# Writing the first stage of a float32 transformer trunk out by hand, pacing a gather, dropping the accumulator clears and halving the tail

## The reference: two macaron layers on 256 tokens

```python
for l in range(2):
    x = x + 0.5 * swiglu(rms_norm(x, ffn1_norm[l]), ffn1_w_gate[l], ffn1_w_up[l], ffn1_w_down[l])
    h = rms_norm(x, mix_norm[l]);  z = h @ w_in[l]          # 1024 -> q | k | v | p, 512 each
    a = neighborhood_attention(q, k, v, rpb[l])             # 8 heads of 64, 2-D windows, learned bias
    m = multiscale_pool(p, w_pool[l], pool_scale[l])
    x = x + concat([a, m]) @ w_out[l]
    x = x + 0.5 * swiglu(rms_norm(x, ffn2_norm[l]), ffn2_w_gate[l], ffn2_w_up[l], ffn2_w_down[l])
return rms_norm(x, final_norm)
# swiglu(h, g, u, d) = (silu(h @ g) * (h @ u)) @ d, with 2816 hidden columns
```

## Time and profile before

| | |
|---|---|
| median of 3 executions | 987.61 us (985.65 to 989.18) |
| profiled execution: span from the first to the last instruction | 983.4 us |
| median less that span (what lies around it) | 4.2 us |
| TensorE busy | 958.7 us, 97% |
| VectorE, ScalarE, GpSimd busy | 552.3, 499.5, 45.1 us |
| DMA | 174.75 MB, mean 178 GB/s |

### The profile page before, as it was taken

One profiled execution on the slowest core, in us unless ns is written; L12 is line 12 of the kernel. 1 busy time (PEld: TensorE's weight loads), 2 busy tenths in 40 slices (PEclk: granted clock), 3 DMA queues, 4 the chain that ended last, 5 costly groups with the idle time before them and its releaser, 6 DMA issues.

```text
span 983.4 us, 13937 instructions
## 1 busy us (share of the span) xinstructions
PE 958.7 (97%) x4390; PEld 780.2 (79%) x4390; DVE 552.3 (56%) x865; ACT 499.5 (51%) x812; POOL 45.1 (5%) x86
## 2 busy tenths in 40 slices
PE   5989999999999999999989999999999999999996
PEld 4878888877788888888878888888868888888885
DVE  4556555467545665554466556564665565465644
ACT  4555455455625654544375545454664365454542
POOL 0550000010001000000010000000100010000000
PEclk9999999999999999999999999999999999999999
DMA  8998646527223746465367555644542266556441
GB/s 285 234 244 284 211 171 212 173 87 250 93 86 129 244 147 210 167 213 171 129 208 254 193 191 171 209 160 143 171 172 86 86 209 199 190 170 213 145 156 43
DMA packets 123269, 174.75 MB, mean 178 GB/s; under 512 B 8240, under 2 KB 99552, under 8 KB 122976
## 3 DMA queue, kind: packets, MB, share of 16 engines
q1 hardware_dynamic: 117328, 165.17, 50.1%
q0 software_dynamic: 2848, 6.38, 3.0%
q10 hardware_dynamic: 3056, 2.75, 0.8%
HBM read 173.14 MB, written 4.19 MB: 180 GB/s over the span
## 4 chain that ended last, share of the span: by engine, by line
issue 92%; POOL 4%; DMA 2%; PE 1%; ACT 0%; ACTq 0%; DVE 0%; POOLq 0%; DVEq 0%; SPq 0%
POOL bias_scratch L364 3%; POOL rstd L337 1%; DMA bias_scratch<-in_rpb_dram 1%; DMA w_raw<-in_ffn_w_up_dram 1%; POOL mean_eps L334 0%; PE ps L868 0%; POOL rstd_scaled L340 0%; PE ps L869 0%; ACT w_hi L416 0%; PE ps L918 0%; ACT L416 0%; POOL bias L371 0%; DVE normed L850 0%; DVEq L95 0%; ACT xt_hi L431 0%
## 5 line engine op out<-in xcount | busy, mean ns | idle before, releaser
L631 DVE SCALAR_TENSOR_TENSOR w_lo<-w_raw,gain,w_hi 128x512 fp32r<-128x512 f32 x416 | 285.4, 746 | 104.3 <-ACT w_hi L416 103.7
L860 PE MATMUL ps<-w_hi,xt_hi 128*128 128x512 f32 x848 | 338.3, 399 | 2.9 <-DVE w_lo L631 2.8
L861 PE MATMUL ps<-w_lo,xt_hi 128*128 128x512 f32 x848 | 330.4, 390 | 0.0
L863 PE MATMUL ps<-w_hi,xt_lo 128*128 128x512 f32 x848 | 326.2, 391 | 0.0
L416 ACT ACTIVATE w_hi<-w_raw,gain 128x512 fp32r<-128x512 f32 x416 | 265.7, 713 | 99.7 <-PE ps L863 78.2
L623 DVE TENSOR_TENSOR w_lo<-w_raw,w_hi 128x1024 fp32r<-128x1024 f32 x104 | 122.7, 1222 | 121.2 <-ACT w_hi L410 121.1
L860 PEld LDWEIGHTS ps<-w_hi,xt_hi 128*128 128x128 f32 x848 | 159.3, 188 | 39.1 <-DVE w_lo L631 4.7
L863 PEld LDWEIGHTS ps<-w_hi,xt_lo 128*128 128x128 f32 x848 | 159.2, 188 | 34.2
L861 PEld LDWEIGHTS ps<-w_lo,xt_hi 128*128 128x128 f32 x848 | 159.6, 188 | 30.4
L410 ACT ACTIVATE w_hi<-w_raw 128x1024 fp32r<-128x1024 f32 x104 | 104.4, 1052 | 105.0 <-PE ps L863 104.3
L860 PE MATMUL ps<-w_hi,gt_hi 128*128 128x512 f32 x352 | 140.0, 398 | 0.0
(11 more groups left out here) (82 smaller groups left out, 468.3 us busy)
## 6 DMA issues: line engine op xcount, KB each, us to landing
w_raw<-in_ffn_w_gate_dram SPq DMA_DIRECT2D x88, 512.0 KB, 4.0
w_raw<-in_ffn_w_up_dram SPq DMA_DIRECT2D x88, 512.0 KB, 5.1
w_raw<-in_ffn_w_down_dram SPq DMA_DIRECT2D x88, 512.0 KB, 4.0
w_raw<-in_w_in_dram SPq DMA_DIRECT2D x32, 512.0 KB, 4.7
w_raw<-in_w_out_dram SPq DMA_DIRECT2D x16, 512.0 KB, 5.2
bias_scratch<-in_rpb_dram POOLq DMA_DIRECT2D x32, 96.0 KB, 6.7
bias<-bias_scratch POOLq DMA_DIRECT2D x2, 1536.0 KB, 8.0
pool_m<-in_pool_matrix_dram ACTq DMA_DIRECT2D x1, 1024.0 KB, 6.5
```

The source lines that it names most:

```text
L631: nc.vector.scalar_tensor_tensor(w_lo[slot][:, part], w_raw[slot][:, part], g, w_hi[slot][:, part].bitcast(F32), ALU.mult, ALU.subtract).t ...
L860: nc.tensor.matmul(o, hi, wh, start=start, stop=False)
L861: nc.tensor.matmul(o, hi, wl, start=False, stop=False)
L863: last = nc.tensor.matmul(o, lo, wh, start=False, stop=stop)
```

## The change

The first gated stage is written out on its own: x is loaded in halves, the weights of chunk 0 in slices (each with its own semaphore), the residual is not added to zeros, both token tiles do the first half of K before the second, and the gains of the first norm are transposed apart from the others. Eight matmuls with zeros stand ahead instead of five. An ACTIVATE with Silu on one column stands ahead of all other work on ACT. The layer loop is a Python loop, so the program is written out for both layers (the chunk loop stays, now from 2). The banks are opened by the first down product of a stage instead of by zeros. The gathers are issued two a chunk, those of layer 0 during its first gated stage, those of layer 1 during its second. Tables and pooling parameters are loaded after the chunk loop of the first gated stage. The second pass enters its first stage with both weight splits on ACT ahead of `xt_hi`. `acc_ready` is raised per bank. In the last stage tile 1 finishes one bank before the other, and the norm behind it is done by halves.

```diff
-            sp.dma_start(resid[:, 0, :], x[0, 0:P, :]).then_inc(x_loaded[0], 16)
-            with sp.Fori(0, DEPTH) as layer:
-                load_ff(layer, FF1, (ffn1_w_gate, ffn1_w_up, ffn1_w_down))
+            def load_first(layer, ff, weights):
+                def quarter(a, k0, k1, q):
+                    slot = ff["g"][a]
+                    dst = w_raw[slot][:, :].rearrange("p (k m c) -> p k m c", k=4, m=2)
+                    for m, w in enumerate(weights[:2]):
+                        src = w[layer, a * 512 + k0 * P:a * 512 + k1 * P, 0:FC]
+                        sp.dma_start(dst[:, k0:k1, m, :], src.rearrange("(k p) c -> p k c", p=P)
+                                     ).then_inc(first_raw[q], 16)
+                sp.dma_start(resid[:, 0, 0:512], x[0, 0:P, 0:512]).then_inc(x_half_loaded, 16)
+                quarter(0, 0, 1, 0)
+                sp.dma_start(resid[:, 0, 512:], x[0, 0:P, 512:]).then_inc(x_loaded[0], 16)
+                for k in range(1, 4):
+                    quarter(0, k, k + 1, k)
+                sp.dma_start(resid[:, 1, :], x[0, P:2 * P, :]).then_inc(x_loaded[1], 16)
+                quarter(1, 0, 2, 4)
+                quarter(1, 2, 4, 5)
+            load_first(0, FF1, (ffn1_w_gate, ffn1_w_up))
+            for layer in range(DEPTH):
+                load_ff(layer, FF1, (ffn1_w_gate, ffn1_w_up, ffn1_w_down), begun=layer == 0)
...
-            for layer in range(DEPTH):
-                for rq in range(P // GRID_W):
-                    for h in range(N_HEADS):
+            def gather_rows(layer, ff, number):
+                for i in range(N_HEADS):
+                    pool.wait_ge(g0_used, chunk_no(layer, ff, i) + 1)
+                    for rq in range(P // GRID_W):
...
+            rstd_of(0)
+            gather_rows(0, FF1, 0)
+            load_bias(0, N_HEADS)
+            rstd_of(1)
+            rstd_of(2)
+            gather_rows(0, FF2, 1)
+            rstd_of(3)
+            load_bias(1, 5)
...
+            load_gain(0)
             act.dma_start(ident[:, :], identity).then_inc(ident_loaded, 16)
+            for j in (1, 2):
+                load_gain(j)
+            act.wait_ge(eps_ready, 1)
+            nc.scalar.activation(table_seed[:, :], eps[:, :], ACT.Silu)
...
+            def first_norm():
+                store_xt_hi(0, 0, 0)
+                act.wait_ge(gains_stored, 1)
+                for k in range(2):
+                    first_hi(k, 0, k)
+                store_xt_hi(0, 0, 1)
+                for k in range(2, 4):
+                    first_hi(k, 0, k)
+                for h in range(2):
+                    store_xt_hi(0, 1, h)
+                squares(0, 0)
+                for k in range(4):
+                    first_hi(4 + k // 2, 1, k)
+                squares(0, 1)
+                act.wait_ge(gains_stored, 2)
...
+                if ff is FF1:
+                    load_params(layer)
+                    if layer == 0:
+                        load_tables()
                 unit_down(layer, ff, LAST - 1)
...
+                    split_hi(*first_unit(layer, FF1, 0), gains_of=(0, layer, 0))
+                    norm(layer, 0, first_unit(layer, FF1, 1), (down_used, down_no(layer, FF1, 1)))
...
+            def first_norm():
+                slots = FF1["g"]
+                store_xt_lo(0, 0, 0)
+                split_lo(slots[0], 0, gains_of=(0, 0, 0), halves=(0,))
+                store_xt_lo(0, 0, 1)
+                split_lo(slots[0], 0, gains_of=(0, 0, 0), halves=(1,))
+                for h in range(2):
+                    store_xt_lo(0, 1, h)
+                split_lo(slots[1], 0, gains_of=(0, 0, 4))
...
+            for h in range(2):
+                add_to_residual(last, 0, h)
+            dve.wait_ge(rstd_ready[0], last + 1)
...
+            for h in range(2):
+                part = slice(h * BANK, (h + 1) * BANK)
+                add_to_residual(last, 1, h)
+                dve.wait_ge(resid_ready[1], 2 * (last - 1) + h + 1)
+                nc.vector.tensor_tensor(z[:, 1, 2 + h, :], resid[:, 1, part], final_gain[:, part],
+                                        ALU.mult).then_inc(gained_ready, 1)
+            for h in range(2):
+                dve.wait_ge(half_sq_ready[h], 1)
+            nc.vector.scalar_tensor_tensor(mean_eps[:, 1:2], half_sq[:, 0:1], eps[:, :],
+                                           half_sq[:, 1:2], ALU.add, ALU.add
+                                           ).then_inc(tail_mean_ready, 1)
...
+            def first_gate_up():
+                for a in range(2):
+                    slot = FF1["g"][a]
+                    for t in range(TT):
+                        if a == 0 and t == 1:
+                            transpose_resid(0, 1)
+                        for k in range(4):
+                            wait_split(slot, 0, k + 1)
+                            if k == 0:
+                                pe.wait_ge(xt_lo_ready, 2 * t + a + 1)
+                            cols = slice(k * BANK, (k + 1) * BANK)
+                            last = split_products(
+                                [ps[:, t, :]], xt_hi[:, t, 4 * a + k, :], xt_lo[:, t, 4 * a + k, :],
+                                [w_hi[slot][:, cols]], [w_lo[slot][:, cols]],
+                                (a, k) == (0, 0), (a, k) == (1, 3))
...
-                for t in range(TT):
-                    clear_acc(t)
+                chunk(layer, ff, 1, True)
+                with pe.Fori(2, LAST) as i:
+                    chunk(layer, ff, i, False)
...
+                    for parts in (((0,), (1,)) if final and t == 1 else ((0, 1),)):
...
-            nc.tensor.matmul(ps[:, 0, :], zeros[:, 0:P], zeros[:, :], start=True, stop=True
-                             ).then_inc(down_used, 1)
-            for t in range(TT):
-                for dh in range(2):
-                    last = nc.tensor.matmul(acc(t, dh), zeros[:, 0:P], zeros[:, :],
-                                            start=True, stop=True)
-                last.then_inc(acc_cleared, 1)
+            for n in range(WARM_UP):
+                last = nc.tensor.matmul(ps[:, n % 2, :], zeros[:, 0:P], zeros[:, :],
+                                        start=True, stop=True)
+            last.then_inc(down_used, 1)
+            pe.wait_ge(ident_loaded, 16)
+            transpose_gains(0).then_inc(gains_t_ready, 1)
+            transpose_resid(0, 0)
+            transpose_gains(1)
+            transpose_gains(2).then_inc(gains_t_ready, 1)
```

377 lines of the change are left out of this document (214 added, 163 removed).

## The result

The changed kernel takes 972.46 us (median of 4 runs, 971.49 to 972.8) against 986.63 for the kernel before beside it (985.23 to 989.18): ratio 0.9845, 95% interval [0.9824, 0.9866]. The profiled execution's span went from 983.4 to 969.5 us, 13.9 less. The prediction said 975.6 (span 971.4), 12.0 less, with 973 to 977.5 as the forecast's own range. The total is 3.1 us off, 1.9 of it in the span, but that hides two larger misses of opposite sign. The other 1.2 us are no part of the kernel: the prediction kept 4.2 us between the span and the median, while an execution takes 1.6 to 2.2 us more than its own span (971.49 and 969.5 for the profiled one).

A forecast was written before the change was run, and what follows sets the result against it. TensorE, busy 97% of the span, bounds the kernel, so gains come from its idle or removable time: -5.6 - 2.4 - 2.4 - 1.5 - 0.1 = -12.0 us, from 987.6 to 975.6. Forecast's own range 973 to 977.5, overall 971.5 to 980.

The forecast's parts named there:

- The start: First gated stage up to chunk 1: first product at 8.8 us, 6.1 earlier; -5.6 us in all, bounds -3.5 and -7.
- I assume the same slow head after the change, so it cancels: First stage: the first products run at half speed (0.42 us apart) before and after, so no gain or loss.
- the rival: First stage: eight matmuls and transposes leave the clock full for the first products; 1.3 us more gain, 974.3; chance 0.25.
- eight at 0.43 end at 5.0, before the identity; cost nothing: Ahead of the first transposes: the warm-up matmuls run while DMA is awaited and add no time.
- The gather: First stage, 35 to 85 us: gathers paced two a chunk stop delaying weights; -2.4 us, bounds 0 and -2.5.
- the gather was not the cause: Early chunks: pacing does nothing and weights wait anyway; 978.0 us, chance 0.05.
- The entry: Entry of layer 1: no loop end, gain copy or table load, splits done earlier; -2.4 us, bounds -1.2 and -2.8.
- the clears: Three later stages without four zeros matmuls: 0.92 less 0.48 us each; -1.5 us in all, bounds -0.5 and -2.8.
- the second split is late for `xt_hi`: Entry of layer 1: the case behind that term's smaller bound, a gain of only -1.2 us.
- The tail: Last norm after TensorE's end, done by halves; -0.1 us, bounds -1 and +0.6.
- the five issues ahead of `unit_down`: Chunk loop's end in layer 0: DMA issues on ACT fit into its wait for TensorE; cost 0, bound +1 us.
- Written-out code: Whole program: rival that engines stall waiting for instructions of the doubled program; 990.6 us and more, chance 0.03.

The follow-up runs named there:

- after_warm1: The changed kernel with one matmul on zeros ahead of the transposes instead of eight; 973.28 us, ratio 0.9850 to the kernel before.
- late_warm1: The changed kernel with gathers held back by two chunks and one zeros matmul instead of eight; 966.64 us, ratio 0.9780 to the kernel before.
- late_gt128: The changed kernel with gathers held back by two chunks and 64 unused bytes on either side of gt_hi and gt_lo; 964.54 us, ratio 0.9764.
- late_gt_plus128: The changed kernel with gathers held back by two chunks and 128 unused bytes ahead of gt_hi; 972.2 us, ratio 0.9840 to the kernel before.
- after_unpaced: The changed kernel with all 32 gathers issued in one row, as before, instead of in pairs; 983.19 us, ratio 0.9953 to the kernel before.

## Why the prediction was right and wrong

Three steps failed, and 972.46 us lies 0.5 below the forecast's own range: the sign of the gather's term (+2.1 for -2.4), a sum that took the distance of the down products as fixed (-4.4 for nothing), and the head of the start (-6.9 for -5.6).

**The start** (-5.6, measured -6.9) was followed correctly up to the first product (8.66 for 8.8), the wait at tile 1 (1.07 for 0.9) and chunk 1's second unit (0.3 us at most for 0.5: 36 products from 14.36, then 24 to 28.08, against 28.38). The step that failed is "I assume the same slow head after the change, so it cancels". The products are 0.23 apart, and from the first product to chunk 1's transposes it takes 19.7 us, where the prediction's terms give 20.9. The rows of before that seemed to speak against the rival had 3.4 us of idle time between transposes and products; after the change it is 1.1, and the runs with one warm-up matmul show that without the eight the head is slow even so. The Trainium skill ("TensorE: Matmul & The Clock Gate", Part 1) has it that sustained activity releases the clock. The trace agrees for one matmul (products 0.43 apart) and for ten of the thirteen executions with eight (0.23); in three the clock was back at half at the first products. And the clock isn't the whole of the 1.3 us: four profiled executions with a slow head (`after_warm1`, `late_warm1`, `late_gt128`, `late_gt_plus128`) have chunk 1's transposes at 28.35 to 28.94, still ahead of the 29.7 that -5.6 gives, with their first product at 7.85 to 8.09. One term that the prediction put at nothing cost 0.6 to 0.7 us at the first product (8.09 and 7.95 with one matmul, 8.66 and 8.65 with eight): "eight at 0.43 end at 5.0, before the identity; cost nothing". In `late_warm1` TensorE had the identity at 4.47, and the eight matmuls held it until 5.18. The slices cost more than forecast, and hardly hurt: ACT got the last quarter at 9.89, not near 8, and waited 0.43 us, and TensorE's product with it started 0.31 us behind the one before, 0.1 more than the distance.

```profile
9.89 0.72 ACT L508 ACTIVATE w_hi<-w_raw,gains 128x512 fp32r<-128x512 f32 x1 [0.43 <-DMA w_raw<-in_ffn_w_up_dram]
```

The prediction's estimate by the Trainium skill ("DMA: Bandwidth & Descriptors", section Bandwidth), which has small transfers slower than large ones, was 9.5; this row bears it out better than my own 8.

**The gather** (-2.4, measured +2.1) is the step that failed by sign. Its bounds were "0 (weights still wait) and -2.5", a loss wasn't among them, although the diff had what was needed: the first pair waits for `g0_used` of chunk 0, which tile 1's first half gives near 17.1 us (12 products from 14.36), before GpSimd's roots are done at 19.7. So that pair isn't paced at all, and goes out 0.3 us behind the first down load (19.71 and 19.39). I took the rows of the kernel before as the cost of the gathers and left the start's term out of it. The two terms weren't independent: pacing is worth 4.6 us in the kernel before (0.0047 of 986) and 10.7 in the changed one (983.19 less 972.46). The rival "the gather was not the cause" is refuted by both.

**The sum lacked a term.** It took the 1,056 down products at the distance that they had. Their distance changed because tensors of other uses changed in size, and this gave 4.4 us, more than any term but the start. That the span came within 1.9 us is luck: +4.5 in the gather against -4.4 here.

**The entry** (-2.4, measured -2.8) and **the clears** (-1.5, measured -1.7) were right in size, and the experiments bear out their parts: 0.5 to 0.6 us a stage for the clears, so of their 0.92 us some 0.35 had covered a wait, where the earlier trace rows gave 0.48. At the entry the prediction credited the missing copy, loop end and table load, and its bound of -1.2 "the second split is late for `xt_hi`" names the part that turned out to be worth 1.3. **The tail** (-0.1, measured 0.0) and the five issues ahead of `unit_down` (0) were right. **Written-out code** brought no wait of TensorE anywhere: between 45 us and the tail its idle times in the timeline sum to 1.4 us, none over 0.25.

## What to carry to other kernels

When two edits touch the same queue, price the second in the timeline that the first leaves, not in the trace of before: here a row of the same gathers cost 3.3 us in one kernel and 18.7 in the other, where it began 6.3 us earlier. Don't let background transfers out beside the first loads that the kernel waits for: here it was enough to hold them back by two chunks, with the semaphore that they wait for unchanged. And read the distance between starts of the commonest instruction in both traces before any idle time: 2% on it, from a buffer that moved, was worth a third of this change.

## What the runs showed of the hardware

- The distance of matmuls (128x512, fp32r, stationary 128x128) depends on where the stationary operand lies relative to the moving one, mod 256 bytes per partition: 0.2267 to 0.2271 us at 0; 0.2288 to 0.2292 at 192; 0.2321 at 128; 0.2329 to 0.2333 at 32, 64 and 224. It held for two tensors, `gt_hi` with six relative places and `xt_hi` with three, and two of the kernels were forecast by it. The weights' raw and split copies share one place mod 256 here, so these runs don't tell whether it is the moving operand or the copies that ACT and DVE work on beside it. The Trainium skill ("TensorE: Matmul & The Clock Gate", Part 2) gives TensorE two independent read ports, so that loading the next stationary operand takes nothing from the running matmul; if the moving operand is what the place is set against, these runs don't agree, by up to 18 us in this kernel (964.54 to 982.68), but that isn't shown.
- With `gt_hi` at 64, the products with `xt_hi`, which stayed at 0, went from 0.2271 to 0.2283 us in three kernels. That is not explained.
- Two gathers of 96 KB from DRAM to DRAM were issued at 19.71 and 20.71 us, beside two loads of 512 KB at 19.39 and 19.94. The first load landed in 5.8 us, the second in 13.9; without the pair the second took 6.8. With fifteen gathers in a row from 19.15 us on, in `after_unpaced`, it took 10.1, so the delay isn't in proportion to the gathers.
- Eight matmuls on zeros from 1.47 us on were followed by full clock at the first products in ten of thirteen profiled executions (0.23 us apart), and by half clock in three (0.43 apart, granted clock 0.50 from about 8 to 11.5 us); one was followed by half clock in both (0.43).
